# A one-core decoder step: the projection's order, constants built earlier, and routing in two steps per head

## The reference, cut to what matters

```python
mod = c @ w_ada + b_ada                      # shift1, scale1, gate1, shift2, scale2, gate2
h   = rms(x) * (1 + scale1) + shift1
z   = h @ w_in                               # q | k | v | forget logits | GLU input (2 x 512)
q, k normalised per head; logf = log_sigmoid(fg + b_f); u = a * sigmoid(b)
A   = forgetting attention (prompt: causal; sampled: over 4 pages of 128 cached rows per sequence)
B   = swish(layernorm(depthwise_conv_31(u)))
x1  = x + gate1 * (concat[A, B] @ w_o)
h2  = rms(x1) * (1 + scale2) + shift2
# PEER, per row: 8 heads; scores against 2 x 128 sub-keys, the 16 best of each half, the 16 best of
# the 16 x 16 sums -> 16 experts of 16384, softmax gates g
act = gelu(h2 . expert_u[eidx]);   y = x1 + gate2 * sum(g * act * expert_v[eidx])
```

## Time and profile before

| what | value |
|---|---|
| median of 3 runs | 3954.36 us (3952.37 to 3976.56) |
| the profiled execution | 3957.28 us, its span 3955.5 us, granted TensorE clock 0.895 of full |
| busy time | PE 3065.7, DVE 2461.9, ACT 1555.4, POOL 1245.4 us |
| moved by DMA | 1291.64 MB, of it 1124.27 MB by GpSimd's gathers |

### The profile page before, as it was taken

The page is one execution under the profiler, slowest core; times in us unless marked ns, Lnnn a source line. Parts: engine busy times, 40 slices in busy tenths (PEclk is TensorE's granted clock), DMA queues, the critical chain, the costliest instruction groups (busy, mean ns, idle before and its releaser), DMA issues. The chain is left out here.

```text
span 3955.5 us, 44026 instructions
## 1 busy us (share of the span) xinstructions
PE 3065.7 (78%) x11624; PEld 1441.8 (36%) x11624; DVE 2461.9 (62%) x6411; ACT 1555.4 (39%) x4273; POOL 1245.4 (31%) x1139
## 2 busy tenths in 40 slices
PE   8799978557786886778688858886888688757876
PEld 2466653332252243224332423252335233411331
DVE  0222222488678668766776777677757775956695
ACT  0233321236524442553354335534552454333433
POOL 0000012023323443433333324433343334334333
PEclk9698889688998998899899979998998799979979
DMA  8211123399998999999999999999999899989998
GB/s 321 81 38 38 38 71 135 129 339 370 382 364 341 412 385 390 366 414 375 370 392 407 394 354 387 398 399 345 399 407 378 337 403 407 391 325 417 410 386 368
DMA packets 299713, 1291.64 MB, mean 327 GB/s; under 512 B 39271, under 2 KB 135415, under 8 KB 163125
## 3 DMA queue, kind: packets, MB, share of 16 engines
q0 software_dynamic: 156672, 1124.27, 70.8%
q1 hardware_dynamic: 142780, 164.51, 12.7%
HBM read 1271.34 MB, written 17.79 MB: 326 GB/s over the span
## 5 line engine op out<-in xcount | busy, mean ns | idle before, releaser
L1660 PE MATMUL YY<-ring,dg 128*64 128x512 f32 (+1 forms) x4224 | 1737.0, 659 | 590.5 <-ACT dg L1231 567.9
L1102 POOL DMA_INDIRECT ring<-experts_dram,idxc x1056 | 1196.4, 1133 | 1917.2 <-PE YY L1660 1701.1
L1505 DVE CUSTOM_DVE_ANT_0 ring<-ring,h2c 128x1024 f32<-128x1024 f32 x1056 | 1265.7, 1224 | 557.4 <-DMA ring<-experts_dram,idxc 548.6
L1660 PEld LDWEIGHTS YY<-ring,dg 128*64 128x64 f32 (+1 forms) x4224 | 517.8, 147 | 1657.8 <-ACT dg L1231 952.3
L1221 ACT ACTIVATE ga<-act 128x1 f32<-128x1 f32 x1056 | 212.5, 201 | 1028.9 <-DVE act L1505 1027.1
L1231 ACT ACTIVATE dg<-fold,gw 128x64 f32<-128x64 f32 x1024 | 356.4, 348 | 50.9 <-PE YY L1660 1.8
L1641 PE MATMUL M<-fT,wq 128*128 128x128 f32 (+1 forms) x2304 | 299.1, 293 | 74.7 <-DMA wq<-w_query_dram 74.6
L1223 ACT ACTIVATE gw<-ga,gc 128x1 f32<-128x1 f32 x1056 | 311.5, 295 | 35.2 <-ACT ga L1221 1.0
L1641 PEld LDWEIGHTS M<-fT,wq 128*128 128x128 f32 x2304 | 290.8, 209 | 79.6 <-DMA wq<-w_query_dram 78.2
L1256 DVE SCALAR_TENSOR_TENSOR yac<-win,cw,yac 128x128 f32<-128x128 f32 x960 | 262.7, 346 | 0.0
L530 PE MATMUL A<-w_in,hT 128*128 128x512 f32 (+1 forms) x432 | 210.7, 652 | 0.0
(11 more groups left out here) (305 smaller groups left out, 2561.0 us busy)
## 6 DMA issues: line engine op xcount, KB each, us to landing
wq<-w_query_dram SPq DMA_DIRECT2D x72, 1024.0 KB, 22.3
wa<-w_ada_dram SPq DMA_DIRECT2D x12, 2048.0 KB, 7.9
ring<-experts_dram,idxc POOLq DMA_INDIRECT x1056, 13.2
w_in<-w_in_dram SPq DMA_DIRECT2D x1, 10272.0 KB, 33.5
kh<-kT_scratch SPq DMA_DIRECT2D x16, 264.0 KB
xb<-x_prompt_dram SPq DMA_DIRECT2D x8, 512.0 KB, 5.2
t_xb<-x_prompt_dram SPq DMA_DIRECT2D x8, 512.0 KB, 11.2
w_o<-w_o_dram SPq DMA_DIRECT2D x8, 512.0 KB, 5.1
```

The lines of the kernel that those rows point to most:

```text
L1102: pool.indirect_dma_start(ring[:, k % RING, :], None, I["experts"], bass.IndirectOffsetOnAxis(idxc[:, k:k + 1], 0)).then_inc(g_in[k % RING ...
L1505: v.tensor_tensor_reduce(out=u, in0=u, in1=h2, scale=1.0, scalar=0.0, op0=ALU.mult, op1=ALU.add, accum_out=act8[:, k % RING:k % RING + 1]) ...
L1660: mm = pe.matmul(YY[o, half * 512:(half + 1) * 512], dg[:, k % DG, 0:w], ring[:, k % RING, D + half * 512:D + (half + 1) * 512], start=(k ...
```

## The change

Five edits.

1. **project, order.** There are two `hT`, and the loops hold two blocks. On TensorE the second GLU half comes first, then `rows_up(t + 1)`, then the first half. The transposes of k go to `A[6]`, `A[7]` (after `hT` of the next block has been read from there), so the forget logits no longer wait for the copies of q and k; q, k, v do. The sampled block's u rows (`u_rows(TS)`) move from between blocks 0 and 1 into block 1.
2. **constants early.** The constants of `sampled`, the page table and `idx` are made at the start of `project`. GpSimd issues the page gathers as the first thing of `sampled`.
3. **routing in two steps.** TensorE multiplies a head's queries in an even step and its scores in the odd one; VectorE's `choose` is cut in two, `shortlist` (the 16 best of each half, even steps) and `choose` (the 16 best sums, odd steps).
4. **groups spread.** Two groups follow each `shortlist` and three each `choose`, in place of five after the whole; six groups are left after the indices are written, not ten. Block 0 has [2] x 12 + [3] x 3 in place of [4] + [5] x 5 + [2, 2] (33 in both).
5. **row copies not behind gates.** ScalarE's `begin` makes the copies of `h2` before it waits for the gates.

```diff
@@ project, TensorE @@
+            def gated(half, r, h):
+                for j in range(half * CC, (half + 1) * CC):
+                    for k in range(DC):
+                        mm = pe.matmul(A[half][:, (j % CC) * P:(j % CC) * P + r],
...
+                mm.then_inc(glu_done, 1)
...
                 pe.wait_ge(hT_ready, t + 1)
+                for k in range(DC):
+                    mm = pe.matmul(A[5][0:r, 0:H], h[:, k, 0:r], w_in[:, k, ZF:ZF + H], start=(k == 0), stop=(k == DC - 1))
+                mm.then_inc(fg_done, 1)
                 if some(t):
                     pe.wait_ge(qkT_ready, t)
...
+                gated(1, r, h)
+                if more:
+                    rows_up(t + 1)
...
+                gated(0, r, h)
                 pe.wait_ge(logf_ready, t + 1)
...
-                if more:
-                    rows_up(t + 1)
                 pe.wait_ge(qk_ready, t + 1)
                 pe.wait_ge(Fq_ready, t + 1)
                 pe.wait_ge(v_ready, t + 1)
+                for i, src in enumerate((qa, ka)):
+                    if i and more:
+                        pe.wait_ge(hT_ready, t + 2)
...
+                            mm = pe.transpose(A[2 + 4 * i + n // 4][0:AUG, (n % 4) * P:(n % 4 + 1) * P],
+                                              src[:, n, :], ident[:, :])
@@ project, start @@
+                             (K["pt"][:, :], I["page_table"].to_broadcast([P, NS * NP]))):
...
-            pool.wait_ge(small_in, 64)
+            pool.wait_ge(small_in, 80)
...
+            v.tensor_scalar(K["idx"][:, :], K["pt"][:, :], float(P), K["lanef"][:, 0:1], ALU.mult, ALU.add)\
+                .then_inc(lane_ready, 1)
@@ sampled, GpSimd @@
-            pool.iota(lane[:, :], [[0, 1]], base=0, channel_multiplier=1).then_inc(cst, 1)
...
-            pool.wait_ge(idx_ready, 1)
             for n in range(NS * NP):
                 pool.indirect_dma_start(pages[:, n, :], None, I["cache"], bass.IndirectOffsetOnAxis(idx[:, n:n + 1], 0))\
@@ tail @@
-S_GATE = S_ROUTE + 3
-STEPS = S_GATE + H + 1
+S_GATE = S_ROUTE + 4
+STEPS = S_GATE + 2 * H
...
-PLAN = [3] * 14 + [4] * 2 + [2, 1, 1, 1, 2, 2, 1, 1, 2, 2, 2, 2] + [2, 1, 1, 1, 1, 2, 2] + [2, 2] + [5] * 7 + [6] + [2, 2]
+PLAN = [3] * 14 + [4] * 2 + [2, 1, 1, 1, 2, 2, 1, 1, 2, 2, 2, 2] + [2, 1, 1, 1, 1, 2, 2] + [3, 3] + [2, 3] * 8 + [2, 1]
...
-PLAN_0 = [0] * (S_GATE + 1) + [4] + [5] * 5 + [2, 2]
+PLAN_0 = [0] * (S_GATE + 1) + [2] * 12 + [3] * 3
@@ tail, ScalarE begin @@
                 if some(e):
+                    fold_h2(e)
                     act.wait_ge(gates_folded, H + e - 1 + P // TS if isinstance(e, int) and e == NB else H + e)
-                    fold_h2(e)
@@ tail, VectorE @@
-            def choose(t, h):
+            def shortlist(t, h):
...
                     own.step(v.max_index(bix[:, g, 8:16], best[:, g, 8:16], sc2[:, g, :]))
+                own.settle()
+
+            def choose(t, h):
...
-                if S_ROUTE + 2 <= s < S_ROUTE + 2 + H:
-                    choose(t, s - S_ROUTE - 2)
+                if S_ROUTE + 2 <= s < S_ROUTE + 2 + 2 * H:
+                    (choose if (s - S_ROUTE) % 2 else shortlist)(t, (s - S_ROUTE - 2) // 2)
```

More of the change, by code:

```diff
@@ L39 @@
 M = 1 + NS
+NP = 4
 EPS = 1e-6
@@ L219, in project @@
         sqq = sb("sqq", [P, 2 * DA])
-        hT = sb("hT", [P, DC, P])
+        hT = [sb(f"hT{i}", [P, DC, P]) for i in range(2)]
         st = sb("st", [P, 8])
@@ L388, in _ @@
             norm_x(0)
-            body(0)
-            with act.Fori(1, NB) as t:
-                body(t)
-            body(NB, False)
+            body(0, 0)
+            body(1, 1)
+            with act.Fori(1, NB // 2) as i:
+                body(2 * i, 0)
+                body(2 * i + 1, 1)
+            body(NB, 0, False)
         @block.vector
@@ L534, in body @@
                     pe.wait_ge(u_ready, t)
-                for j in range(2 * CC):
-                    for k in range(DC):
-                        mm = pe.matmul(A[j // CC][:, (j % CC) * P:(j % CC) * P + r],
-                                       w_in[:, k, ZG + j * P:ZG + (j + 1) * P], hT[:, k, 0:r],
-                                       start=(k == 0), stop=(k == DC - 1))
-                mm.then_inc(glu_done, 1)
+                if isinstance(t, int) and t == 1:
+                    u_rows(TS)
+                gated(1, r, h)
+                if more:
+                    rows_up(t + 1)
+                if isinstance(t, int) and t == 1:
+                    pe.wait_ge(ubs_ready, 1)
+                gated(0, r, h)
                 pe.wait_ge(logf_ready, t + 1)
@@ L570, in _ @@
             rows_up(0)
[L571 to L577 removed]
+            body(0, 0)
+            body(1, 1)
+            with pe.Fori(1, NB // 2) as i:
+                body(2 * i, 0)
+                body(2 * i + 1, 1)
+            body(NB, 0, False)
             pe.wait_ge(u_ready, NB + 1)
@@ L594, in sampled @@
         KT = sb("KT", [P, 2, CC, NP * P])
-        idx = sb("idx", [P, NS * NP], I32)
-        pt = sb("pt", [P, NS * NP], I32)
-        lane = sb("lane", [P, 1], I32)
-        lanef = sb("lanef", [P, 1])
+        idx, later, later32, upto = K["idx"], K["later"], K["later32"], K["upto"]
+        hrow, hcol, ones5, Qbd = K["hrow"], K["hcol"], K["ones5"], K["Qbd"]
         qT = sb("s_qT", [P, CC, TS])
@@ L703, in _ @@
             own = Own(v, own_v)
-            v.wait_ge(pt_in, 16)
-            v.wait_ge(cst, 8)
-            own.do(v.tensor_copy(lanef[:, :], lane[:, :]))
-            v.tensor_scalar(idx[:, :], pt[:, :], float(P), lanef[:, 0:1], ALU.mult, ALU.add).then_inc(idx_ready, 1)
             v.wait_ge(small_in, 64)
@@ L1189, in step @@
                                    ACT.Copy).then_inc(sc_ready, 1)
-                if s == S_GATE + H - 1 and some(t):
+                if s == STEPS - 2 and some(t):
                     act.wait_ge(sh_ready, H + t)
                     act.activation(ge[:, :, :], ge[:, :, :], ACT.Exp).then_inc(eg_ready, 1)
-                if S_GATE <= s < S_GATE + H and not some(t):
-                    h = s - S_GATE
+                if S_GATE <= s < S_GATE + 2 * H and (s - S_GATE) % 2 == 0 and not some(t):
+                    h = (s - S_GATE) // 2
                     act.wait_ge(sh_ready, h + 1)
@@ L1447, in step @@
                     modulate(r)
-                if S_ROUTE + 2 <= s < S_ROUTE + 2 + H:
-                    choose(t, s - S_ROUTE - 2)
-                if s == S_ROUTE + 1 + H and some(t):
+                if S_ROUTE + 2 <= s < S_ROUTE + 2 + 2 * H:
+                    (choose if (s - S_ROUTE) % 2 else shortlist)(t, (s - S_ROUTE - 2) // 2)
+                if s == S_ROUTE + 1 + 2 * H and some(t):
                     write_indices(t)
-                if S_GATE < s <= S_GATE + H and not some(t):
-                    h = s - S_GATE - 1
+                if S_GATE < s < S_GATE + 2 * H and (s - S_GATE) % 2 and not some(t):
+                    h = (s - S_GATE) // 2
                     v.wait_ge(eg_ready, h + 1)
@@ L1463, in step @@
                     v.sem_inc(gates_folded, 1)
-                if s == S_GATE + H and some(t):
+                if s == STEPS - 1 and some(t):
                     write_gates(t)
-                if s == S_ROUTE + H + 2 and smp:
+                if s == STEPS - 2 and smp:
                     v.wait_ge(idx_ready, FOLD * FOLD * (8 + t))
@@ L1713, in build @@
             K[name] = ctx.enter_context(nc.sbuf_tensor(name, shape, F32))
-        with ExitStack() as early:
-            for name, shape in (("tri", [P, P]), ("ones", [P, P]), ("w_in", [P, DC, DIN])):
-                K[name] = early.enter_context(nc.sbuf_tensor(name, shape, F32))
-            condition(nc, I, S, K, w_in_load)
-            project(nc, I, O, S, K, w_in_load)
-        sampled(nc, I, O, S, K)
+        with ExitStack() as paged:
+            for name, shape, kind in (("idx", [P, NS * NP], I32), ("pt", [P, NS * NP], I32), ("lane", [P, 1], I32),
+                                      ("lanef", [P, 1], F32), ("later", [P, 896], F32), ("later32", [TS, TS], F32),
+                                      ("upto", [TS, NS, QS], F32), ("hrow", [H, P], F32), ("hcol", [H, DA], F32),
+                                      ("ones5", [TS, 512], F32), ("Qbd", [P, CC, NS, H, QS], F32)):
+                K[name] = paged.enter_context(nc.sbuf_tensor("k_" + name, shape, kind))
+            with ExitStack() as early:
+                for name, shape in (("tri", [P, P]), ("ones", [P, P]), ("w_in", [P, DC, DIN])):
+                    K[name] = early.enter_context(nc.sbuf_tensor(name, shape, F32))
+                condition(nc, I, S, K, w_in_load)
+                project(nc, I, O, S, K, w_in_load)
+            sampled(nc, I, O, S, K)
         tail(nc, I, O, S, K)
```

136 lines of the change are left out of this document (62 added, 74 removed).

## The result

The changed kernel takes 3871.26 us (median of 4 runs, 3867.27 to 3873.22) against 3956.71 us; the ratio is 0.9771, 95% interval 0.9743 to 0.9799. Measured again on another chip, it is 0.9762 (0.9735 to 0.9789). The forecast was 3856 us, so the sum of 98.5 us came out as 85.

| stretch | before, us | after, us | won | forecast |
|---|---|---|---|---|
| project, first operation on GpSimd to the last transposes of u | 443.77 | 404.49 | 39.3 | 44.5 |
| from there to tail's first operation (sampled) | 121.64 | 117.75 | 3.9 | 6 |
| tail | 3266.9 | 3226.5 | 40.4 | 48 |

A forecast was written before the change was run, and what follows sets the result against it. TensorE was taken to bound project, DMA tail, and VectorE the first block's routing. Terms 45 + 6 - 0.5 + 3 + 20 + 25 = 98.5 us took the profiled 3957.3 to 3858.8, a predicted median of 3856, range 3805 to 3900.

The forecast's parts named there:

- The step of the gaps and the clock: Project's seams: gaps of 3.26 us shrink to 0.4 and 0.5 and the clock stays up, winning 45 us.
- Rival C: Project: the gaps shrink but the clock still falls behind each, 70 us won, 3884 us; chance 0.06.
- One issue more, 0.37 us: Project's start: the page table's DMA ahead of GpSimd's wait; early constants there taken as -0.5 us, bounds 0 and -3.
- Sampled: Start of sampled: page gathers issued first there bring the pages earlier, 6 us won, bounds 5 and 6.1.
- the 33 groups and eight heads are the same work: Tail's first block: VectorE starts 3 us earlier (bounds 0 and 4.2), and its work behind that is unchanged.
- All 4.9 us are won: Tail's three loop seams: the earlier first dot counts in full, 15 us of the seams' 20.
- up to 4 us at each of eight seams if the ring holds landed data: Tail's routing: a loss from indices coming with six groups left, not ten; 1 us taken per seam.
- Cut in two, with two and three groups between: Tail's routing: the longest pause falls to 5.5 us, winning 33 us, half of some 66 idle; net 25.
- Rival B: Tail's routing: spreading groups wins nothing, as a ring of eight transfers covers the pauses; 3881 us, chance 0.18.
- the added settle ... 0: Tail's routing: the added `settle`, 72 times under 0.2 us on an engine not the bound there, costs 0.
- D: Tail: the even flow wins most idle DMA, routing 60 and seams 30 us; 3811 us, chance 0.16.
- E: Tail: `wq` loads land late beside unpaused gathers; 4072 us, decisive from 1.2 us per head; chance 0.04.

The follow-up runs named there:

- copies_back: The changed kernel with edit 5 undone, ScalarE's copies again behind the wait for the gates: 3879.45 us, ratio 0.9794.
- in_fives: The changed kernel with a head's groups together, none after `shortlist` and five after `choose` in blocks 1 to 8: 3866.61 us, ratio 0.9750.
- plan_alone: The kernel before with edit 5 and the group counts of in_fives, routing in the old order: 3947.68 us, ratio 0.9954.
- the two runs: The kernel before with edit 5 alone (3937.54 us, ratio 0.9937), and copies_back.

## Why the prediction was right, and where it was not

**What bounds the kernel.** Right. In the fourteen profiled executions (before, changed and the twelve runs) tail's length less its idle DMA lies between 3013 and 3030 us, and most of what is won is idle DMA: 236.6 us over the whole of tail before, 205.3 after, 31 of the 40.4 us. The other 9 lie within the 17 us by which that remainder differs between executions.

**Project.** The step of the gaps and the clock is right: the sum's 45 us over seven blocks come to 6.4 a block, and a block took 41.0 us in place of 47.8, and the gaps of 0.4 and 0.5 us are 0.52 and 0.51. The rule of the Trainium skill that was set against it (TensorE: Matmul & The Clock Gate, "A second HAM failure mode: psum-queue depth-cycling") could, as the prediction read it, have kept the clock down behind the short gaps. The trace doesn't show that here: it has 1.00 over five blocks. Rival C is out. Two terms were mis-sized. "One issue more, 0.37 us" priced the page table's issue and not its landing: GpSimd's wait was put over five loads in place of four, with ScalarE's first square behind it. It cost 2.0 us, and 0.65 more beside GpSimd's selects. And the first two blocks run partly at the lower clock in both kernels, for a time that differs between executions of the same code: the second block begins 66.4 to 66.8 us behind the stage's start in four executions with the changed project and 69.7 in two others, the one of the result among them. In the four, project is 400.6 to 401.1 us long in place of 404.5, and 43 us are won. What makes the difference stays open.

**Sampled.** The first page came as much earlier as reckoned. That TensorE would meet it at the lower clock was left out.

**First block.** 3 us at its place, and the step "the 33 groups and eight heads are the same work" is what failed behind it: the work is the same, but in the new order VectorE waits 2.91 us for a later head's scores and 1.42 us for a gather, so that the 33rd dot is 2.5 us late. At the 128th dot four executions of the changed tail lie between 524.6 and 530.2 us behind the stage's start (531.3 before), a spread wider than the term.

**Seams.** "All 4.9 us are won" is right of the step, and nearly of the price: 17 to 18 us of idle DMA by the two runs against 20. The failing step is the one set against the routing: "up to 4 us at each of eight seams if the ring holds landed data ... I take 1 us each". In place of its 8 us the runs show 38.2 less 24.3, 14 us, with the first gather of a new block 4 us earlier (16.1 against 12.3 us ahead of the gates).

**Routing.** A net of 25 us was forecast; without the early copies the idle DMA of the seven blocks falls by 16 (117.9 to 102.2). The reason given for it is wrong. "Cut in two, with two and three groups between, the longest pause is the 5.5 us of the new choose ... I take half, 33 us" names the spread as what wins. The idle time outside the seams' thirty microseconds did fall, from 93.5 us to 68.6 (64.1 in copies_back), 25 to 29 us against the 33 forecast, but in_fives keeps the whole pause and has 22 of it (71.6 us). Rival B's premise, that a ring of eight covers the pauses, is right, and its time is wrong, because the same edit also changed the order of the queries and scores. That part had been given no price at all: "the added settle ... 0" is all that was said of edit 3 on the other engines. plan_alone shows what is missing without it. So it is in part luck that tail came out near its sum: a cause priced at 33 us won nothing, and one that had no price took its place.

**The other rivals.** D: the even flow won no more than the uneven. E: TensorE's waits for `wq` rose from 74.7 to 96.3 us, 0.3 us a head, far below the 1.2 from which it would decide.

## What to carry to other kernels

Where one resource bounds, count its idle time by place before and after. An edit that fills it at one place empties the queue for the next: the copies were worth 17 us and showed 4, because the edit beside them had the ring's gathers begun earlier, so that they ended earlier in the pause at the seam. Price every part of an edit, the reorder that only makes room too: here it won, and the even spread that it was made for did not. A new load put on an old semaphore makes all who wait on it wait for its landing.

## What was not expected of the hardware

- Work that comes earlier can meet the lower clock: page transposes of 1.12 in place of 0.66 us at a granted clock of 0.59, which gave back 1.6 of 5.6 us. In ten executions with the early gathers nine met it.
- The clock's price behind a gap isn't one sum: nothing behind 0.5 us, 1.8 us of lost time behind 2.3, up to 4.9 behind 3.26.
- A hardware loop's branch shows as 4.3 to 5.1 us on VectorE and 4.8 to 5.6 on ScalarE at each seam, with work in hand on both; the six blocks written out won some 20 us.
- While GpSimd makes its selects, four small operations of VectorE take 1.30 us in place of 0.72; two of them, of two inputs, take 0.29 and 0.58 in place of 0.15.
